# Loads of x ahead of all else, zero writes behind the convolution tiles, and an overlapped first norm in a hybrid trunk kernel

## The reference

```python
h = concatenate([meta, x])
for i in range(2):
    hn = rms_norm(h, norm_mix_pre[i])
    m = deltanet_stickbreak_mixer(hn, ...) if i == 0 else s5_mixer(hn, ...)
    h = h + rms_norm(m, norm_mix_post[i])
    f = (silu(hn2 @ w_gate) * (hn2 @ w_up)) @ w_down      # hn2 = rms_norm(h, norm_ffn_pre[i])
    h = h + rms_norm(f, norm_ffn_post[i])
return h[:, 16:]
```

## Time and profile before

| | |
|---|---|
| median of 3 runs | 3239.78 us (3233.03 to 3246.63) |
| profiled execution | 3224.44 us, span 3222.7 us |
| busy share: PE, PEld, DVE, ACT, POOL | 89%, 85%, 39%, 22%, 29% |
| mean granted TensorE clock | 0.953 of full |
| DMA traffic | 236.31 MB, mean 73 GB/s |
| PE busy in the first 32 us, in the next 44 us | 0.00 us, 20.26 us |
| DMA share in the first 32 us | 0.95, at 310 GB/s |

### The profile page before, as it was taken

How to read it: one execution, slowest core, us unless ns; L and a number is a source line. 1 busy time by engine, 2 the same in 40 slices (tenths; PEclk the granted TensorE clock), 3 DMA queues, 4 the chain that set the end, 5 groups by cost and what they waited for, 6 DMA issues and landing times.

```text
span 3222.7 us, 44723 instructions
## 1 busy us (share of the span) xinstructions
PE 2870.7 (89%) x17885; PEld 2733.7 (85%) x17885; DVE 1250.6 (39%) x2090; ACT 698.0 (22%) x1183; POOL 948.5 (29%) x390
## 2 busy tenths in 40 slices
PE   3999987875899999999999988457999999999996
PEld 2999976765678899999999978347989999999996
DVE  1665135553541444445543340361044222332234
ACT  3222134342543400000110142121052000000002
POOL 2343400000004344343334223102443334534330
PEclk8999989897999999999999989678999999999998
DMA  5122520001111222222213123793122111111102
GB/s 165 67 85 102 113 79 26 26 26 47 40 36 58 92 65 100 67 73 73 67 67 110 41 81 82 183 213 93 59 93 86 46 39 44 54 46 46 45 27 70
DMA packets 175487, 236.31 MB, mean 73 GB/s; under 512 B 56480, under 2 KB 140960, under 8 KB 173088
## 3 DMA queue, kind: packets, MB, share of 16 engines
q1 hardware_dynamic: 66064, 133.42, 14.0%
q10 hardware_dynamic: 109328, 101.54, 10.1%
HBM read 172.37 MB, written 62.55 MB: 73 GB/s over the span
## 4 chain that ended last, share of the span: by engine, by line
issue 34%; PE 30%; POOL 12%; DVE 9%; DMA 6%; ACT 4%; ACTq 2%; SPq 1%; POOLq 0%; DVEq 0%
POOL w_hi L576 8%; PE psum L604 5%; PE psum L605 5%; PE psum L606 5%; POOL w_lo L580 4%; DMA stage<-wstream 4%; PE psum L662 3%; DVE area L1796 2%; PE psum L848 2%; PE psum L981 2%; PE psum L840 1%; PE psum L953 1%; DVE area L1720 1%; DVE area L1725 1%; DMA area<-xT 1%
## 5 line engine op out<-in xcount | busy, mean ns | idle before, releaser
L604 PE MATMUL psum<-x_hi,w_hi 128*128 128x344 f32 (+2 forms) x3600 | 1165.1, 324 | 54.7 <-DVE x_lo L1743 26.9
L605 PE MATMUL psum<-x_lo,w_hi 128*128 128x344 f32 (+2 forms) x3600 | 1158.7, 322 | 0.0
L606 PE MATMUL psum<-x_hi,w_lo 128*128 128x344 f32 (+2 forms) x3600 | 1153.8, 320 | 0.0
L576 POOL TENSOR_TENSOR w_hi<-stage,const 128x1024 fp32r<-128x1024 f32 x193 | 470.0, 2435 | 2169.0 <-PE psum L606 2145.6
L604 PEld LDWEIGHTS psum<-x_hi,w_hi 128*128 128x128 f32 x3600 | 680.8, 189 | 62.7 <-DVE x_lo L1743 26.7
L605 PEld LDWEIGHTS psum<-x_lo,w_hi 128*128 128x128 f32 x3600 | 679.9, 189 | 1.9
L606 PEld LDWEIGHTS psum<-x_hi,w_lo 128*128 128x128 f32 x3600 | 681.0, 189 | 0.0
L580 POOL TENSOR_TENSOR w_lo<-stage,w_hi 128x1024 fp32r<-128x1024 f32 x193 | 482.6, 2500 | 15.1
L604 PE MATMUL psum<-act_hi,w_hi 128*128 128x344 f32 (+1 forms) x1056 | 347.3, 329 | 22.1 <-DVE area L2076 16.7
L606 PE MATMUL psum<-act_hi,w_lo 128*128 128x344 f32 (+1 forms) x1056 | 341.9, 324 | 0.0
L605 PE MATMUL psum<-act_lo,w_hi 128*128 128x344 f32 (+1 forms) x1056 | 341.0, 323 | 0.0
(11 more groups left out here) (212 smaller groups left out, 2400.0 us busy)
## 6 DMA issues: line engine op xcount, KB each, us to landing
stage<-wstream SPq DMA_DIRECT2D x193, 512.0 KB, 3.5
s_set<-area ACTq DMA_DIRECT2D x8, 1860.0 KB, 8.0
proj<-area ACTq DMA_DIRECT2D x28, 520.0 KB, 2.6
area<-proj ACTq DMA_DIRECT2D x40, 256.0 KB, 4.3
resid<-area ACTq DMA_DIRECT2D x6, 1376.0 KB, 6.1
area<-resid ACTq DMA_DIRECT2D x6, 1376.0 KB, 8.4
area<-proj ACTq DMA_DIRECT2D x12, 520.0 KB, 5.1
area<-xT ACTq DMA_DIRECT2D x4, 1376.0 KB, 8.7
```

The lines of the kernel that those rows point to most:

```text
L576: pool.tensor_tensor(per_block(w_hi[:, slot, :]), per_block(stage[:, h, :]), all_ones, ALU.mult).then_inc(high_split, 1)
L604: mm(out[:, 0:n], w_hi[:, slot, wk], hi[:, xk, a:a + n], start=first, stop=False)
L605: mm(out[:, 0:n], w_hi[:, slot, wk], lo[:, xk, a:a + n], start=False, stop=False)
L606: return mm(out[:, 0:n], w_lo[:, slot, wk], hi[:, xk, a:a + n], start=False, stop=last)
```

## The change

- `const` is loaded in two parts. SP issues, ahead of all weight slabs: blocks 0 and 1 (identity and ones), `small`, the second and third parts of x, and the other 19 blocks of `const` (`N_CONST_USED` is `N_CONST`). ACT's first instruction is the load of the first part of x. The third part has an h buffer of its own (`first_h`).
- The second third has its own `sq` buffers and its own bank for the sums (6), so the sums wait less for each other: sum 1 for nothing but its squares, sum 2 for `nm_normed` 1.
- ACT squares third 1 ahead of root 0 and third 2 ahead of root 1; DVE does `norm_pre` of a third ahead of `norm_low` of the one before.
- Three of the memsets, among them that which raises `gate_dve`, move ahead of the first norm.
- The five zero writes move from ACT's start to behind the convolution loop.

```diff
--- before.py
+++ after.py
@@ -374,6 +375,7 @@
         nm_loaded = [sem(f"nm_loaded{i}") for i in range(2)]
+        first_loaded = [nm_loaded[0], nm_loaded[1], sem("first_loaded")]
         nm_square = sem("nm_square")
@@ -423,6 +425,11 @@
         norm_sums = bank[7]
+        first_h = [nv["h"][0], nv["h"][1], carve(3 * T_ROWS, KT, 344)]
+        halves_of = lambda x: [x[:, 4 * i:4 * i + 4] for i in range(2)]
+        sq_halves = halves_of(nv["sq"])
+        first_sq = [sq_halves, [carve(3 * T_ROWS + KT * 344, 4, 344), carve(A1 + 3 * KT * CW, 4, 344)], sq_halves]
+        first_sums = [bank[7], bank[6], bank[7]]
         DOWN_BANKS = 3
@@ -532,6 +539,13 @@
+            sp.dma_start(const[:, 0:2 * P], const_in[:, 0:2 * P]).then_inc(params_loaded, 16)
+            sp.dma_start(small[:], small_in).then_inc(params_loaded, 16)
+            for c in (1, 2):
+                a, n = CUTS[c]
+                sp.dma_start(first_h[c][:, :, 0:n], xT[:, :, a:a + n]).then_inc(first_loaded[c], 16)
+            sp.dma_start(const[:, 2 * P:N_CONST_USED], const_in[:, 2 * P:N_CONST_USED]).then_inc(zeros_written, 16)
@@ -649,8 +663,10 @@
                 e = norm_event(r, c, m)
-                if r == 0 and c:
-                    pe.wait_ge(nm_normed, c)
+                sums, sq = (first_sums[c], first_sq[c]) if r == 0 else (norm_sums, sq_halves)
+                if r == 0:
+                    if c == 2:
+                        pe.wait_ge(nm_normed, 1)
                 elif r == 4 and c:
@@ -659,7 +675,7 @@
                         pe.wait_ge(nm_square, 2 * e + k // 4 + 1)
-                    last = mm(norm_sums[:, 0:n], ones, nv["sq"][:, k, 0:n], start=(k == 0), stop=(k == KT - 1))
+                    last = mm(sums[:, 0:n], ones, sq[k // 4][:, k % 4, 0:n], start=(k == 0), stop=(k == KT - 1))
                 last.then_inc(nm_sum, 1)
@@ -1111,6 +1127,8 @@
                     act.wait_ge(nm_stored[0], 16 * 7)
+                elif r == 0:
+                    pass
                 elif c == 2:
@@ -1121,24 +1139,27 @@
                 e = norm_event(r, c, m)
+                sq = first_sq[c] if r == 0 else sq_halves
                 if r == 0:
-                    act.wait_ge(nm_loaded[c % 2], 16 * (c // 2 + 1))
+                    act.wait_ge(first_loaded[c], 16)
                 elif m:
...
                     act.wait_ge(*acc_complete(r, c))
-                x = nv["h"][c % 2][:, :, 0:n] if m else acc[:, :, a:a + n]
-                if e:
+                x = first_h[c][:, :, 0:n] if r == 0 else nv["h"][c % 2][:, :, 0:n] if m else acc[:, :, a:a + n]
+                if r == 0 and c == 2:
+                    act.wait_ge(nm_sum, 1)
+                elif r:
                     act.wait_ge(nm_sum, e)
...
                     ks = slice(4 * half, 4 * half + 4)
-                    A(nv["sq"][:, ks, 0:n], x[:, ks], ACT.Square).then_inc(nm_square, 1)
+                    A(sq[half][:, :, 0:n], x[:, ks], ACT.Square).then_inc(nm_square, 1)
...
                 e = norm_event(r, c, m)
-                rs = norm_sums[:, 0:n]
+                rs = (first_sums[c] if r == 0 else norm_sums)[:, 0:n]
                 act.wait_ge(nm_sum, e + 1)
@@ -1157,21 +1178,11 @@
                 act.wait_ge(nm_normed, 3 * r + c + 1)
-                A(x_hi[:, :, a:a + n], nv["h"][c % 2][:, :, 0:n], ACT.Copy).then_inc(nm_high, 1)
-            act.dma_start(small[:], small_in).then_inc(params_loaded, 16)
-            act.dma_start(const[:], const_in).then_inc(params_loaded, 16)
+                h = first_h[c] if r == 0 else nv["h"][c % 2]
+                A(x_hi[:, :, a:a + n], h[:, :, 0:n], ACT.Copy).then_inc(nm_high, 1)
+            norm_load(0, 0)
             act.wait_ge(eps_ready, 3)
-            zeros = carve(18300, T_PAD - T)
-            for g in range(4):
-                act.dma_start(proj[7 * g:7 * g + 7, :, T:T_PAD].rearrange("m p t -> p m t"),
-                              zeros.rearrange("p (a t) -> p a t", a=1).to_broadcast([P, 7, T_PAD - T])
-                              ).then_inc(zeros_written, 16)
-            no_lag = (LAGS - CH) * G_CH
-            act.dma_start(s5_k.rearrange("c m g w -> c (m g) w")[:, :, CH * G_CH:LAGS * G_CH],
-                          zeros[0:G_CH, 0:no_lag].rearrange("p (a t) -> p a t", a=1).to_broadcast([G_CH, KT * GPT, no_lag])
-                          ).then_inc(zeros_written, 16)
@@ -1179,17 +1190,13 @@
                 act.sem_inc(u_stored[i], 16)
-            act.wait_ge(params_loaded, 32)
-            norm_load(0, 0)
-            norm_load(0, 1)
             norm_square(0, 0, 1)
+            norm_square(0, 1, 1)
             norm_root(0, 0, 1)
-            norm_square(0, 1, 1)
+            norm_square(0, 2, 1)
             norm_root(0, 1, 1)
             norm_high(0, 0)
-            norm_load(0, 2)
             norm_high(0, 1)
-            norm_square(0, 2, 1)
             norm_root(0, 2, 1)
@@ -1250,6 +1257,15 @@
                 conv_tiles(i)
+            zeros = carve(18300, T_PAD - T)
+            for g in range(4):
+                act.dma_start(proj[7 * g:7 * g + 7, :, T:T_PAD].rearrange("m p t -> p m t"),
+                              zeros.rearrange("p (a t) -> p a t", a=1).to_broadcast([P, 7, T_PAD - T])
+                              ).then_inc(zeros_written, 16)
+            no_lag = (LAGS - CH) * G_CH
+            act.dma_start(s5_k.rearrange("c m g w -> c (m g) w")[:, :, CH * G_CH:LAGS * G_CH],
+                          zeros[0:G_CH, 0:no_lag].rearrange("p (a t) -> p a t", a=1).to_broadcast([G_CH, KT * GPT, no_lag])
+                          ).then_inc(zeros_written, 16)
             act.wait_ge(s5["params"], 16)
@@ -1285,7 +1301,7 @@
             act.wait_ge(s5["tab_stored"], 16 * 13)
-            act.wait_ge(zeros_written, 80)
+            act.wait_ge(zeros_written, 96)
             act.wait_ge(cols_done, 1)
@@ -1709,7 +1725,7 @@
                 dve.wait_ge(nm_root, norm_event(r, c, m) + 1)
-                return norm_sums[:, 0:CUTS[c][1]]
+                return (first_sums[c] if r == 0 else norm_sums)[:, 0:CUTS[c][1]]
@@ -1721,13 +1737,13 @@
                 ch.sync()
-                dve.wait_ge(nm_loaded[c % 2], 16 * (r + 1 if c == 1 else 2 * r + c // 2 + 1))
+                dve.wait_ge(nm_loaded[c % 2], 16 * (r + 1 if c == 1 else 2 * r + c // 2))
                 V.tensor_tensor(h, h, acc[:, :, a:a + n], add).then_inc(nm_resid, 1)
...
                 n = CUTS[c][1]
-                h, rr = nv["h"][c % 2], norm_scale(r, c, 1)
+                h, rr = first_h[c] if r == 0 else nv["h"][c % 2], norm_scale(r, c, 1)
                 if r > 0:
@@ -1740,7 +1756,8 @@
                 dve.wait_ge(nm_high, 3 * r + c + 1)
-                V.tensor_tensor(x_lo[:, :, a:a + n], nv["h"][c % 2][:, :, 0:n], x_hi[:, :, a:a + n].bitcast(F32), sub
+                h = first_h[c] if r == 0 else nv["h"][c % 2]
+                V.tensor_tensor(x_lo[:, :, a:a + n], h[:, :, 0:n], x_hi[:, :, a:a + n].bitcast(F32), sub
                                 ).then_inc(x_ready, 1)
@@ -1750,25 +1767,29 @@
                     dve.sem_inc(s_, 1)
-            dve.wait_ge(params_loaded, 32)
-            for c in range(3):
-                norm_pre(0, c)
-                norm_low(0, c)
...
             ga, gb, keep = carve(T_ROWS, T_ROWS), carve(2 * T_ROWS, T_ROWS), carve(3 * T_ROWS, T_ROWS)
-            cb, ct, po = conv_views(carve)
             ch(V.memset(rows, 0.0))
...
+            ch.sync()
+            V.memset(gb, 0.0).then_inc(gate_dve, 1)
+            dve.wait_ge(params_loaded, 32)
+            norm_pre(0, 0)
+            norm_pre(0, 1)
+            norm_low(0, 0)
+            norm_pre(0, 2)
+            norm_low(0, 1)
+            norm_low(0, 2)
+            cb, ct, po = conv_views(carve)
+            dve.wait_ge(x_ready, 3)
             ch(V.memset(keep, 1.0))
...
             ch.sync()
-            V.memset(gb, 0.0).then_inc(gate_dve, 1)
             dve.wait_ge(gate_act, 1)
```

More of the change, by code:

```diff
@@ L79 @@
 N_CONST = P * 21
+N_CONST_USED = N_CONST
 LEVELS = 7
```

## The result

The median of the first runs fell from 3236.41 to 3202.89 us (four runs each; 3229.75 to 3246.63 before, 3191.76 to 3208.24 after), a ratio of 0.9889 with a 95% interval of 0.985 to 0.9928. Two repetitions gave 0.9923 (0.9897 to 0.9949; 3230.30 to 3209.52) and 0.9937 (0.9917 to 0.9957; 3227.89 to 3206.77). Between the two profiled executions the span fell by 19.8 us. The forecast was 27.4 us. So the change is worth some 20 us, 0.6%; the 33.5 us of the first medians are more than either repetition (20.8, 21.1) or the traces show, and the scatter of single runs is large enough for that. The medians alone can hardly tell 20 from 27 us (27.4 is a ratio of 0.9915, inside one of the two repetitions' intervals and just outside the other's); what was wrong is read from the traces.

What follows compares the result with a forecast made beforehand. TensorE, busy 89% of the span, was taken as the bound, so time is gained only where it idles or is held. -38.7 + 9.3 + 2.0 = -27.4 us, 3239.8 to 3212; range 3201 to 3226, forecast alone 3207 to 3217.

Steps and rivals of the forecast that it cites:

- the first term: From the first convolution tap on, the chain that sets the end runs 38.7 us earlier.
- The ladder of the norm: First norm, step by step: first square near 11.0 us, x_ready steps at 35.3, 45.4 and 48.4.
- I take 1.5 for both: Before the gates' end at 58.0: 0 to 2.4 us for a cold clock plus 0 to 2.3 for POOL splits.
- The port: POOL splits hold DVE operations with two SBUF inputs: 0 to 2.3 us on `norm_low`, 1.0 lost in gate arithmetic.
- The loop as the chain that sets the end: Convolution loop: the chain of waits, 38.7 us earlier, sets the end; TensorE is more held than pushed.
- The jitter of 2: Convolution loop: 2 us either way, since each tile has one or two taps held by a split.
- The zero writes: Behind the convolution loop: five issues on ACT, hidden by nothing, cost 9.3 us, ends 3.1 and 13.5.
- The cold start: TensorE behind the convolution loop, idle about 12 us: a lowered clock costs 2.0 us more, ends 0 and 2.4.
- Rival A: Behind the convolution loop: zero writes nearly hidden, 3.1 us, clock mostly kept; -34.6 us, 3205; chance 0.16.
- Rival B: Behind the convolution loop: zero writes block ACT 18 to 23 us; -19 to -14, 3221 to 3226; chance 0.11.
- Rival C: Front gives less: x's first third takes 15.2 us again (+5), port +3; -19 us, 3220; chance 0.10.
- the rest shifts as a whole: Everything behind the zero writes and cold start: all rows simply 27 us earlier than before.

Runs made afterwards that it cites:

- first trace: First profiled execution of the changed kernel as it is, against the kernel before: span 3202.9 us against 3222.7.
- first two traces: Profiles of the changed kernel as it is, first measurement and first repetition: spans 3202.9 and 3211.3 us; the repetition's median 3209.52 us, ratio 0.9923.
- third trace: Profile of the changed kernel, unaltered, measured a third time: 3206.77 us, ratio 0.9937 to the kernel before, span 3200.4.
- zeros_late: Changed kernel with the five zero writes moved from behind the convolution loop to behind plain_tiles(4): 3198.08 us, ratio 0.9898 to the kernel before.
- second trace of the kernel before: Kernel before, unaltered, measured against itself with a second profile: ratio 1.0004, span 3223.4 us.
- warm: Changed kernel plus fillers, unread matmuls, eight behind the norm's third sum and eight ahead of the second third's gates: 3198.90 us, ratio 0.9905 to the kernel before.

## Why the prediction was right or wrong

The sum was -38.7 + 9.3 + 2.0 = -27.4. In the first trace it is -28.5 (last store of the loop) + 8.05 + 1.6 - 0.9 (all that follows) = -19.8. Nearly the whole difference is the first term.

- **The ladder of the norm: right.** First square forecast 11.0, found 9.65; x_ready 1 forecast 35.3, the gates began at 35.35; x_ready 3 forecast 48.4, found 50.2, later by splits of POOL.
- **The step that failed: "the gates of the second third follow about 4 us of idleness: 0 to 2.4", and "I take 1.5 for both".** The clock was priced from a sum, where it came back in the middle; the gates were taken to do the same. They did not: the clock stayed at 0.50 through all six of them. The gates ended at 66.1 instead of 58.0, 8.1 us, and the fillers gave 10 us back. The prediction also looked only at the idle time ahead of the second third. Its own ladder has as much ahead of the first (the third sum starts at about 26 and takes under 5 us, x_ready 1 comes at 35.3); there the clock fell, and at 0.50 the first third's gates fill the time until x_ready 2, so that the idle time that was priced never came. Nothing in the trace of before contradicted the assumption, because there the gates began right behind a sum that had raised the clock; that they had never been seen starting at the low clock was the gap.
- **The port: right as a mechanism, too small in the gate arithmetic.** The two later `norm_low` lost 2.5 us, hidden by the slow gates. The gate arithmetic lost 3.3 (31.4 us earlier at the last drain, 28.1 at the first tap), where 1.0 was taken. The rule of the Trainium skill (SBUF — State Buffer, "SBUF: two separate sides") names both sides of it, and the trace agrees: the two 3 us operations of DVE stretch the splits too, from 2.4 to 5.1 us.
- **The loop as the chain that sets the end: right in the first two traces**, where the first tap's 28.1 became 28.5 at the last store. The jitter of 2 was far too small for one execution in three: in the third trace the loop was 15 us shorter.
- **The zero writes: right in the first two traces.** 9.3 forecast, 8.05 found. The cold start, 2.0 forecast and 1.6 found, has the right size, but it is not the writes' price: zeros_late and the second trace of the kernel before have it behind waits of 2.7 and 2.6 us. Rival A was refuted for this place in the first trace and shown for another one; in the third trace it held here as well, because the loop had become the faster side. Rival B did not occur behind the loop, but its size did at the front (22.5 us); that a full queue is the reason is not shown.
- **Rival C** came nearest to the size (-19), by luck: at the first tap the front gave 10.6 us less than the 38.7 of the forecast, and not by the landing of x, which was earlier than taken, but by the clock and in a small part by the port.
- **All behind**: -0.9 us in the first trace, up to some 15 in the third, 13 of them with the clock at 0.50 in one stretch of the DeltaNet phase. The forecast that "the rest shifts as a whole" holds for one execution and not for another.

## What to carry to other kernels

When a wait is shortened, look at what the removed work did for TensorE's clock: here a sum that used to run right ahead of the gate tiles had brought it up, and without it a phase of 17 us took 31. Price a phase at both levels if its shapes have only been seen at one. And a blocking DMA issue has no price of its own: the same five issues blocked ACT for 22.5, 8.05 and 9.8 us and cost the path 16.6, 8 and 0 us, by what the issuing engine owes to others at that moment; put them where its consumers have room.

## What the runs showed of the hardware that was not expected

- The gate tiles ran for 31 us without a gap at a granted clock of 0.50 when they began behind idle time, and at 1.00 when they began behind a sum or fillers (the kernel before, warm). The clock rose in the fillers and in the projection's tiles that followed.
- The same wait of 2.6 or 2.7 us behind the convolution loop left the clock at 1.00 in one execution of the kernel before; in the other the clock fell, which cost 1.4 us.
- A loop in which DVE taps and POOL splits hold each other has more than one rhythm: 11.9 us a tile in twelve traces, 10.7 in one, which ran the same program as two of the twelve.
- The zero writes block ACT for 22.5 us when x is being loaded on both queues, 13.5 behind `const`, 8.05 to 9.8 later.
